# Spatial constants built during the first slabs, first slab computed by column tile, samples' query and key rows spread by transfer

## What is computed

```python
mod = silu(c) @ w_ada + b_ada                        # 6 rows of 1024 for each of 9 conditions
h = rmsnorm(x, g_norm1) * (1 + sc1) + sh1
q, k, vm, o, ig, fg, u, vs = split(h @ w_in)         # 4 heads x 128 each, two gates for each head
h_ml, C, n, m = mlstm(q, k, vm, ig + b, fg + b, C0, n0, m0)   # matrix memory, chunks of 128
h_ml = rmsnorm(h_ml, g_head) * sigmoid(o)
vs = layernorm(gelu(vs), ln_g, ln_b)
h_cm = gelu(u) * (tril(w_s) @ vs + b_s)              # spatial gate inside chunks of 128
x = x + gt1 * (concat(h_ml, h_cm) @ w_out)
h2 = rmsnorm(x, g_norm2) * (1 + sc2) + sh2
x = x + gt2 * ((silu(h2 @ w_gate) * (h2 @ w_up)) @ w_down)
y = rmsnorm(x, g_final)
```

## Time and profile before

| what | us |
|---|---|
| median of 3 runs | 2568.75 (2564.78 to 2570.92) |
| the profiled execution, its own time | 2567.24 |
| its span, first to last instruction | 2565.6 |
| PE busy | 2484.3 |
| DVE busy | 1203.4 |
| ACT busy | 846.5 |
| POOL busy | 161.5 |

### The profile page before, as it was taken

One profiled execution on the slowest core, in us unless ns is written; L12 is line 12 of the kernel. 1 busy time (PEld: TensorE's weight loads), 2 busy tenths in 40 slices (PEclk: granted clock), 3 DMA queues, 4 the chain that ended last, 5 costly groups with the idle time before them and its releaser, 6 DMA issues.

```text
span 2565.6 us, 32860 instructions
## 1 busy us (share of the span) xinstructions
PE 2484.3 (97%) x12360; PEld 1996.8 (78%) x12360; DVE 1203.4 (47%) x1759; ACT 846.5 (33%) x1148; POOL 161.5 (6%) x130
## 2 busy tenths in 40 slices
PE   4999999999999999999999999999989999999997
PEld 2678777788888788888888888888857877777775
DVE  4557544434337554444336554444365754333323
ACT  2243322233244243333244243333244323333211
POOL 0022000000004000000003000000002300000000
PEclk8999999999999999999999999999989999999998
DMA  7732545332342243332242233332333222222222
GB/s 270 247 102 84 173 149 157 92 100 99 99 125 67 94 123 94 94 101 94 89 140 74 95 115 94 95 98 91 103 118 107 79 73 75 82 81 81 85 89 75
DMA packets 358691, 275.93 MB, mean 108 GB/s; under 512 B 10992, under 2 KB 302356, under 8 KB 358567
## 3 DMA queue, kind: packets, MB, share of 16 engines
q1 hardware_dynamic: 330500, 224.57, 29.4%
q10 hardware_dynamic: 24116, 34.95, 4.0%
q0 software_dynamic: 3968, 14.95, 1.5%
HBM read 263.49 MB, written 10.96 MB: 107 GB/s over the span
## 4 chain that ended last, share of the span: by engine, by line
PE 85%; DVE 8%; issue 2%; DMA 2%; ACT 2%; ACTq 1%; POOL 0%; DVEq 0%; POOLq 0%; SPq 0%
PE banks L1751 17%; PE banks L1752 17%; PE banks L1753 17%; PE banks L1804 8%; PE banks L1806 8%; PE banks L1805 8%; PE banks L1765 1%; PE banks L1629 1%; DVE w_lo L1263 1%; DMA raw<-in_w_in_dram 1%; ACT w_hi L784 1%; PE banks L1775 1%; PE banks L1879 1%; DVE hT_lo L1269 1%; DVE x L1591 1%
## 5 line engine op out<-in xcount | busy, mean ns | idle before, releaser
L1751 PE MATMUL banks<-hT_hi,w_lo 128*128 128x512 f32 x2176 | 868.2, 399 | 11.0 <-DVE w_lo L1263 8.5
L1752 PE MATMUL banks<-hT_lo,w_hi 128*128 128x512 f32 x2176 | 853.3, 392 | 0.0
L1753 PE MATMUL banks<-hT_hi,w_hi 128*128 128x512 f32 x2176 | 852.4, 392 | 0.0
L1263 DVE TENSOR_TENSOR w_lo<-raw,w_hi 128x1024 fp32r<-128x1024 f32 x392 | 480.4, 1226 | 646.9 <-ACT w_hi L784 635.7
L784 ACT ACTIVATE w_hi<-raw 128x1024 fp32r<-128x1024 f32 x392 | 412.6, 1053 | 470.8 <-PE banks L1806 442.7
L1751 PEld LDWEIGHTS banks<-hT_hi,w_lo 128*128 128x128 f32 x2176 | 412.1, 189 | 115.9 <-issue 15.5
L1753 PEld LDWEIGHTS banks<-hT_hi,w_hi 128*128 128x128 f32 x2176 | 411.6, 189 | 88.2
L1752 PEld LDWEIGHTS banks<-hT_lo,w_hi 128*128 128x128 f32 x2176 | 412.2, 189 | 81.3
L1804 PE MATMUL banks<-w_lo,act_hi 128*128 128x512 f32 x704 | 277.2, 394 | 0.0
L1806 PE MATMUL banks<-w_hi,act_hi 128*128 128x512 f32 x704 | 274.2, 390 | 0.0
L1805 PE MATMUL banks<-w_hi,act_lo 128*128 128x512 f32 x704 | 274.1, 389 | 0.0
(11 more groups left out here) (332 smaller groups left out, 1880.4 us busy)
## 6 DMA issues: line engine op xcount, KB each, us to landing
raw<-in_w_gate_up_dram SPq DMA_DIRECT2D x176, 512.0 KB, 3.7
raw<-in_w_in_dram SPq DMA_DIRECT2D x96, 512.0 KB, 3.8
raw<-in_w_down_dram SPq DMA_DIRECT2D x88, 512.0 KB, 3.7
ada_stage<-in_w_ada_dram ACTq DMA_DIRECT2D x8, 2048.0 KB
raw<-in_w_out_dram SPq DMA_DIRECT2D x32, 512.0 KB, 3.7
in_stage<-in_w_in_dram ACTq DMA_DIRECT2D x6, 2048.0 KB
stage<-in_w_ada_dram SPq DMA_DIRECT2D x4, 2048.0 KB
x_sb<-in_x_prompt_dram POOLq DMA_DIRECT2D x4, 2048.0 KB, 9.0
```

The costliest lines, as they stand in the source:

```text
L1263: ve.tensor_tensor(w_lo[:, s % 2], raw[:, s % 2], w_hi[:, s % 2].bitcast(F32), ALU.subtract).then_inc(lo_done.sem, 1)
L1751: mm(out, w_lo[:, slot, k, :], rhs_hi[:, r, :], start=start and n == 0, stop=False)
L1752: mm(out, w_hi[:, slot, k, :], rhs_lo[:, r, :], start=False, stop=False)
L1753: ins = mm(out, w_hi[:, slot, k, :], rhs_hi[:, r, :], start=False, stop=stop and last)
```

## The change

Five things are done in another place or by another engine.

1. At the start POOL issues the load of `x_sb` first and masks `w_s` after the root; the loads of `w_s`, `ln_b`, `b_s` and the gates' bias are issued by ACT after the first slab's split, that of `g_final` in step 8. The spatial constants are made in steps 0 to 2 of block 0's window, in bank T[0]. PE does `thin(2)`, then the first half of `first_norm`, then `thin(3)`; DVE does `modulation(2)`, the diagonals, the split of the gate weights, `modulation(3)`. The samples' norm moves one step back.
2. `first_products` makes the gates and slab 0 of block 0 tile by tile, each tile as soon as `h_ready` tells it; `FIRST_NORM_BANK` keeps the gates' bank free.
3. In block 0's up stage the first load of `in_stage` is issued after the first pair, one for each pair from there on, and each `thin` runs one pair later; the last, of 8 columns, has its own row `proj_gates`.
4. In the last block POOL issues the five small loads, and scales the state C0 (8 operations of 128x512) after `wv_set`.
5. `sel8` and PE's q and k matmuls go. `load_qk` reads a sample's q and k row from `proj_rows` with a broadcast over 128 partitions (two loads of 256 KB); samples 0 and 1 in step 4, sample b + 1 when ACT begins sample b. DVE and ACT read the rows from SBUF, and DVE does three operations a sample. The pieces are spread over the steps anew.

```diff
-SAMPLES = {2: ("SG",), 3: ("SW", "SB"), 4: ("SC", "SV"), 5: ("C0", "SH", "C1"), 6: ("C2",),
-           7: ("C3", "C4"), 8: ("C5", "C6"), 9: ("C7",), 10: ("SQ",), 11: ("ST", "SN"), 12: ("SX",)}
+SAMPLES = {2: ("SG",), 3: ("SW",), 4: ("SB", "SV"), 5: ("SC", "C0"), 6: ("SH", "C1"), 7: ("C2", "C3"),
+           8: ("C4", "C5"), 9: ("C6", "C7"), 10: ("SQ",), 11: ("ST", "SN"), 12: ("SX",)}
...
+        FIRST_NORM_BANK = [SP_, N1, N2, T[0]]
...
+        def thin_rows(t):
+            return proj_gates[0:NB, :] if t == TH_IN + N_TH_IN - 1 else proj_row
+        def load_qk(engine, b):
+            for dst, c in ((q_all, Q0), (k_all, K0)):
+                engine.dma_start(dst[b % 2][:, :], proj_rows[b:b + 1, c:c + HW].broadcast_to([P, HW]))\
+                    .then_inc(qk_in[b % 2].sem, 16)
...
+            pool.dma_start(x_sb[:, :, :], x_v[0]).then_inc(x_in.sem, 16)
...
+            pool.sem_inc(x1_free.sem, 1)
+            root(0, -1)
            pool.wait_ge(sem("ws_in"), 16)
...
                 if last:
+                    pool.wait_ge(x1_free.sem, x1_free.at(blk, 1))
+                    for dst, src, single in ((sm["bg"][:, :], b_gate.broadcast_to([NB, 2 * H]), False),
+                                             (sm["m0"][:, :], state_m[0], False),
+                                             (n0[:, :, :], state_n[0], False),
+                                             (sm["w00"][:, :], w_s[:, :, 0, 0].broadcast_to([NB, H]), True),
+                                             (sm["bs0"][:, :], b_s[:, :, 0].broadcast_to([NB, H]), True)):
+                        pool.dma_start(dst, src, allow_slow_non_contiguous=single).then_inc(sem("state_in"), 16)
                     pool.wait_ge(sem("vars"), 1)
                     power(sem("rvs"), sm["rv"][:, :], sm["var"][:, :], H, NB)
+                    pool.wait_ge(sem("C_in"), 16)
+                    pool.wait_ge(sem("wv_set"), 1)
+                    for b in range(NB):
+                        pool.tensor_tensor(C0[:, b], C0[:, b], each_head(colq[:, 13, :, b]), ALU.mult)\
+                            .then_inc(sem("C_scaled"), 1)
...
-            fetch("ws_in", w_raw[:, :, :], w_s[0].rearrange("h t s -> t h s"))
-            act.wait_ge(sem("constants_set"), 1)
-            fetch("cmb_in", lnb_lh[0:1, :, :], ln_b)
-            fetch("cmb_in", cmb_rh[1:2, :, :], b_s)
             act.wait_ge(sem("constants_set"), 2)
             gcols = gw_raw[:, 0:KT * 36].rearrange("p (k c) -> p k c", c=36)
             fetch("gw_in", gcols[:, :, 0:H], in_v[:, :, GATE0:GATE0 + H])
             fetch("gw_in", gcols[:, :, 32:32 + H], in_v[:, :, GATE0 + H:GATE0 + 2 * H])
-            act.wait_ge(sem("constants_set"), 3)
-            fetch("gb_in", gb[0:H, :], b_gate[0, 0:H].rearrange("(h o) -> h o", o=1))
-            fetch("gb_in", gb[32:32 + H, :], b_gate[0, H:2 * H].rearrange("(h o) -> h o", o=1))
-            fetch("gf_in", g_fin[:, :], g_final.rearrange("(o d) -> o d", o=1).broadcast_to([P, D]))
...
-                    act.wait_ge(sem("qkb"), b + 1)
+                    act.wait_ge(qk_in[b % 2].sem, 32 * (b // 2 + 1))
                     if b > 0:
                         act.wait_ge(sem("C_upd"), b)
+                    if 1 <= b < NB - 1:
+                        load_qk(act, b + 1)
                     for h in range(H):
-                        ins = act.activation(tmp[:, HW + h * P:HW + (h + 1) * P], K_BANK[b][:, h * P:(h + 1) * P],
+                        ins = act.activation(tmp[:, HW + h * P:HW + (h + 1) * P], k_all[b % 2][:, h * P:(h + 1) * P],
...
+                        if first and step == 8:
+                            fetch("gf_in", g_fin[:, :], g_final.rearrange("(o d) -> o d", o=1).broadcast_to([P, D]))
                         if first and step + N_ADA0 + 1 in range(N_ADA0 + 2, N_ADA):
                             load_ada(step + N_ADA0 + 1)
-                        if last:
-                            load_samples(blk, step)
+                        if last and step == 0:
+                            load_samples()
+                        if last and step == 4:
+                            act.wait_ge(x1_free.sem, x1_free.at(blk, 1))
+                            for b in range(2):
+                                load_qk(act, b)
...
-                    for t in (TH_IN, TH_IN + 1):
-                        load_thin_in(t)
                     for pair_i in range(N_TH_IN + 1):
-                        if pair_i > 0:
-                            store_thin_in(TH_IN + pair_i - 1)
-                            if pair_i + 1 < N_TH_IN:
-                                load_thin_in(TH_IN + pair_i + 1)
+                        if 2 <= pair_i:
+                            store_thin_in(TH_IN + pair_i - 2)
+                        if pair_i == N_TH_IN:
+                            store_thin_in(TH_IN + N_TH_IN - 1)
                         gate_pairs(pair_i)
+                        if pair_i < N_TH_IN - 1:
+                            load_thin_in(TH_IN + pair_i)
+                        if pair_i == N_TH_IN - 2:
+                            load_thin_in(TH_IN + N_TH_IN - 1)
...
-            act.wait_ge(sem("small_set"), 4)
             split_hi(0, 0, used=False)
+            fetch("ws_in", w_raw[:, :, :], w_s[0].rearrange("h t s -> t h s"))
+            fetch("cmb_in", lnb_lh[0:1, :, :], ln_b)
+            fetch("cmb_in", cmb_rh[1:2, :, :], b_s)
+            act.wait_ge(sem("constants_set"), 3)
+            fetch("gb_in", gb[0:H, :], b_gate[0, 0:H].rearrange("(h o) -> h o", o=1))
+            fetch("gb_in", gb[32:32 + H, :], b_gate[0, H:2 * H].rearrange("(h o) -> h o", o=1))
...
+            modulation(2)
+            mean_square(0, -1)
+            ve.tensor_tensor(dg[:, :, :], ident[:, :].unsqueeze(1).broadcast_to([P, TT, P]),
+                             each_head(rrt[:, :]), ALU.mult).then_inc(sem("small_set"), 1)
             ve.wait_ge(sem("gw_in"), 32)
...
-                    ve.tensor_copy(sel8[:, :, :], each_head(ident[0:NB, 0:NB])).then_inc(sem("constants_set"), 1)
                     ve.wait_ge(sem("proj_in"), 16)
-                    ve.wait_ge(sem("srow_in"), 128)
+                    ve.wait_ge(sem("srow_in"), 48)
+                    ve.wait_ge(sem("state_in"), 80)
...
-                    ve.wait_ge(sem("qkb"), b + 1)
-                    Qb = Q_BANK[b][:, :].rearrange("p (h d) -> p h d", h=H)
+                    ve.wait_ge(qk_in[b % 2].sem, 32 * (b // 2 + 1))
+                    ve.wait_ge(sem("C_scaled"), b + 1)
+                    Qb = q_all[b % 2][:, :].rearrange("p (h d) -> p h d", h=H)
                     t0 = tmp[:, 0:HW].rearrange("p (h d) -> p h d", h=H)
                     t1 = tmp[:, HW:2 * HW].rearrange("p (h d) -> p h d", h=H)
                     link(ve.tensor_tensor(t0, C0[:, b], Qb, ALU.mult))
-                    ve.tensor_reduce(colq[:, 2, :, b], t0, AX.X, ALU.add)
-                    link(ve.tensor_tensor(C0[:, b], C0[:, b], each_head(wiT[:, :, b]), ALU.mult))
...
+                            spatial_constants(step)
+                            if step == 3:
+                                ve.wait_ge(sem("gb_in"), 32)
+                            if step == 2:
                                 link(sample_norm("ss1s", "ms1s", "r1s", g1b[:, :]))
                                 modulate(0, 1, "h1s")
                             if N_ADA0 <= step + 3 < N_ADA:
                                 modulation(step + 3)
-                            if step == 3:
+                            if step == 4:
...
+            def spatial_constants(step):
+                if step == 0:
+                    pe.wait_ge(sem("ws_masked"), 1)
+                    pe.wait_ge(h32.sem, h32.at(0, 0))
+                    for h in range(H):
+                        ins = pe.transpose(T[0][:, h * P:(h + 1) * P], w_raw[:, h, :], ident[:, :])
+                    ins.then_inc(sem("small_ps"), 1)
+                elif step == 1:
+                    pe.wait_ge(sem("small_set"), 4)
+                    mm(T[0][0:1, :], onecol[:, :], wT[:, :, :].rearrange("s h t -> s (h t)"), start=True, stop=True)\
+                        .then_inc(sem("small_ps"), 1)
+                elif step == 2:
+                    pe.wait_ge(sem("small_set"), 5)
+                    pe.wait_ge(sem("cmb_in"), 32)
+                    for h in range(H):
+                        ins = mm(T[0][:, h * P:(h + 1) * P], lnb_lh[:, h, :], cmb_rh[:, h, :], start=True, stop=True)
+                    ins.then_inc(sem("small_ps"), 1)
+                elif step == 3:
+                    pe.wait_ge(sem("small_set"), 6)
...
+            thin(2, hTs, R, BLK)
+            pe.wait_ge(sem("small_set"), 2)
             first_norm(range(4))
-            for t in range(2, N_ADA0):
-                thin(t, hTs, R, BLK)
+            thin(3, hTs, R, BLK)
...
-                elif step[0] == "C":
-                    b = int(step[1])
-                    if b == 0:
```

(65 more changed lines are left out.)

81 lines of the change are left out of this document (27 added, 54 removed).

## The result

The changed kernel takes 2550.74 us (median of 4 runs, 2548.67 to 2553.45) beside 2568.11 for the kernel before on that chip: ratio 0.994, interval 0.9923 to 0.9957. On another chip it was 2551.66 beside 2565.24, 0.9949 (0.9935 to 0.9962). It is faster, by 13 to 17 us; 11.5 were forecast.

The account below looks back on a forecast made before the run. PE, busy 97% of the span, was taken as the bound, with time to be had only where it waits, does removable work or runs at half clock. 9.4 − 3.5 + 6.6 − 1.0 = 11.5 us off gave a 2557 us median, range 2546 to 2565.

Parts of the forecast that it names:

- Start: Program's start up to slab 0: constants' round trips and the gates' wait go, so slab 0 ends 9.4 us earlier.
- My bound of 13 us: Upper bound of the gain at the program's start, if `thin(2)` and `first_norm` run at full clock.
- Block 0's window: Spatial constants return as 2.6 us of PE work, and PE's wait in step 2 grows to 1.7 us: loss 3.5.
- Up stage: Block 0's first up pair falls from 30.55 to 23.97 us with fewer pieces issued ahead: gain 6.6 us.
- Last block: Last block's window: removing 15 us of PE work gains nothing, as waits move to DVE, POOL and loads; 1.0 us lost.
- Step (5): Last block: PE starts slab 11 1 us earlier, but at half clock, 7.9 us for 5.5: 1 us lost.
- the estimate with POOL first at every turn: Last block: by the skill's exclusion rule alone, POOL's eight scalings would cost VectorE 8.4 us, forecast 1.4 us later.
- (A): The whole forecast as summed: median 2557 us, own range 2552 to 2561; chance 0.52.
- (B): Rival: the last block gains too, contention taken away moving the gate columns 6 us forward; 2549 to 2552 us; chance 0.22.
- (C): Rival: the start gains only 4 us because the third `w_ada` piece lands at 31; 2562 or 2563 us; chance 0.13.
- (D): Rival: slower than before through four chained `load_qk` loads, each microsecond above 4.7 costing 4; 2576 at 9.5 us; chance 0.08.
- (E): Rival: change 3 or 2 does nothing, slab loads being late for another reason; 2564 us; chance 0.05.

Follow-up runs that it names:

- four_pairs: The changed kernel with four q and four k buffers instead of two each, rows asked for three samples ahead: 2547.91 us, ratio 0.9932 to the kernel before.
- last_undone: The changed kernel with the last block's part taken back (q and k broadcast by matmul, scalings on DVE, small loads on ACT's queue): 2551.66 us, ratio 0.9951.
- after_again: The changed kernel itself, unchanged, run and profiled a second time: 2551.66 us, ratio 0.9949 to the kernel before.

## Why the prediction was right, step by step

**Start, 9.4 forecast, 7.6 measured.** The mechanism was right, two sizes were off. The third piece's product began at 26.61, not 25.2, and `first_norm` took 6.08 us, not 5.31, so the norm tiles came at 48.09, not 46.4 (6.0 us gained of 7.6). The wait of the gates was worth 1.68 of 1.83. In `four_pairs` the third piece's product took 1.90 us in place of 3.45, and there slab 0 came at 64.44, the forecast 9.4 us earlier: a quicker product made up for a later piece, which is luck. The rate I took from the earlier trace rows was the slow one of two. My bound of 13 us took that rate for a low clock; the granted clock of that row is 1.00, as it is over the 3.45 and over the 1.90 us, so by these rows the clock is not the reason, and which rate comes stays open.

**Block 0's window, −3.5 forecast, −2.1 measured.** PE's part was right (2.38 for 2.6). The step that failed is the wait: DVE's copy, norm and modulation took 7.95 us (83.62 to 91.57) for the 9 forecast, and PE waited 0.60 us for them, not 1.7.

**Up stage, +6.6 forecast, 3.5 to 7.2 measured**, 5.7 by taking it back. The cause in the earlier trace rows was right; the price is a stall of 3.2 us plus what the clock takes, and the one profile of before that I had gave this at its highest.

**Last block, −1.0 forecast; nothing by taking it back, +3.3 against the profile of before.** Most of its steps held. Behind the first `v` slab the gates' sum came 0.4 us later (0.9 forecast). POOL's scalings cost DVE 6.2 us (1.38 waited, and 0.75, 0.86 and 3.17 on three instructions) for 7 forecast. The q and k loads of samples 2 to 7 took 4.0 to 5.0 us, both issues included, for 4.7. PE restarted at the lower clock behind the gate columns: from their copy to the evacuation of slab 11 it took 9.04 us at 0.69 granted, and 8.32 at 1.00 in the earlier trace rows's trace. Step (5) has a slip: 7.9 us for 5.5 from a start 1 us earlier is 1.4 us lost, not 1.0. One transfer fewer stood in the chain than forecast, since the load of sample 5 was issued at 1924.78 while ACT's gate weights still ran. The gate columns came 92.9 us behind the first `v` slab, 93.6 with the old code in `last_undone`, 97.0 in the profile of before: where half a microsecond late was forecast, they are 0.7 early. What failed is the basis: I took the profile of before as what its code costs, and that stretch ran at 0.83 where the same code elsewhere had 0.90.

The Trainium skill, "SBUF — State Buffer", section "Who interferes with whom", has VectorE's two-input instructions and GpSimd's reads exclude each other, and reductions and ScalarE untouched. The trace agrees in most: the reduction kept its 0.69 us, and ScalarE's scalings left the scans at 1.36. One two-input addition at 1894.89 took 0.70 while POOL ran, so not every turn is lost: 6.2 us were measured, where 8.4 was the estimate with POOL first at every turn.

**Sum.** 11.5 were forecast, and 16.9 lie between the profiles. Parts taken back give 5.6 (start and first window), 5.7 (up stage) and 0 (last block), so 11.3 us; by the timed ratios, each good to about 0.001, 0.0026, 0.0021 and 0.0002 of 2565 us, 12.6 of the 13.1 that `after_again` has. So the forecast is right for the code, with some luck: its four terms missed by −1.8, +1.4, −0.9 and +1.0 us, which nearly cancel. The profile's further 5.6 us lie in before's last window (3.3), up pair (1.5) and the rest (0.8), the first two where its granted clock was lower. The measured median, 2550.74, lies below (A)'s own range (2552 to 2561) and in (B)'s, though not for (B)'s reason. One point stays open: why both profiles of before had the lower clock in the last window. Of the rivals, (C), (D) and (E) fell: the start gave its part, the loads in the chain took 5.0 us at most, and changes 2 and 3 gave 1.68 and 5.7 us. (B) put the contention at 6 us; it was not absent, as (B) has it, but paid, and taking it away gave 3.7, as the loads came last then.

## What to carry to other kernels

Work taken off a full engine gives nothing when the chain that replaces it is longer: 16.3 us less of PE's busy time in the last window (`last_undone` to after) came back as 16.4 us in which PE stood still, and only shortening that chain (scalings off POOL, deeper buffers, the awaited work first) gave 3 to 4 us each. Take a change back part by part in the final kernel and compare stretches, not spans. Before pricing a stretch by one profile, look at its granted clock: four profiles of the same code differed by up to 4.8 us, more than the change made in that stretch.

## What was not expected of the hardware

With PE busy 50.00 of 50 us in four profiles of the same code the granted clock was 0.80 to 0.90, and the window 109.39 to 114.18 us long. The same product of 16 matmuls took 3.45 and 1.90 us, both at a granted clock of 1.00, at the start of two kernels whose starts are the same code. Four scans of 4x128 took 4.53 us for 1.36 beside POOL's series: about one POOL operation (9.81 us for eight, 1.23 each) for each scan.
